# A hybrid encoder layer: the pre-expert weights as 1 MB units in four rotating slots, the first expert gathered transposed, the residual products in the last steps

## The reference, cut to what matters

```
h = rmsnorm(x);  proj = h @ w_in + b_in          # q, k, v, lru-x, lru-gate, merge gates
A = grouped-query attention (8 heads of 64, 2 kv heads, rotary positions)
R = conv4 -> forward and backward gated linear recurrence, summed, times gelu(lru-gate)
x += (sigmoid(gA) * (A @ W_A) + sigmoid(gR) * (R @ W_R)) @ W_out
t = rmsnorm(x);  logits = t @ w_router + b_router
x += sum over the top 4 of 32 experts of gate * (swiglu(t @ w_gu[e] + b_gu[e]) @ w_down[e] + b_down[e])
out = rmsnorm(x)
```

## Time and profile before

| what | value |
|---|---|
| runs | 1136.24, 1137.75, 1137.98 us; median 1137.75 |
| span of the profiled execution, first to last instruction | 1134.2 us |
| around the span (median less span) | 3.55 us |
| TensorE / VectorE / ScalarE busy | 1084.8 / 371.1 / 237.2 us |
| bytes moved by DMA | 439.77 MB, mean 388 GB/s |
| stage before the experts | 0 to 226 us; 32 experts from there on |

### The profile page before, as it was taken

One profiled execution on the slowest core, in us unless ns is written; L12 is line 12 of the kernel. 1 busy time (PEld: TensorE's weight loads), 2 busy tenths in 40 slices (PEclk: granted clock), 3 DMA queues, 4 the chain that ended last, 5 costly groups with the idle time before them and its releaser, 6 DMA issues.

```text
span 1134.2 us, 12887 instructions
## 1 busy us (share of the span) xinstructions
PE 1084.8 (96%) x5407; PEld 503.4 (44%) x5407; DVE 371.1 (33%) x645; ACT 237.2 (21%) x369; POOL 2.6 (0%) x10
## 2 busy tenths in 40 slices
PE   7999999999999999999998989898989899899987
PEld 7999899633333333333333333333333333333332
DVE  6997887522212222122121211111211212121212
ACT  5399961211111111111111110011110101010102
POOL 0000000000000000000000000000000000000000
PEclk9999999899999999999999999999999999999999
DMA  9544277999999999999999999999999999999996
GB/s 353 185 178 149 84 287 300 419 425 399 431 425 428 426 434 432 433 426 435 431 429 436 430 430 436 429 430 436 430 432 433 429 436 430 427 427 429 426 428 247
DMA packets 25637, 439.77 MB, mean 388 GB/s; under 512 B 3425, under 2 KB 4065, under 8 KB 6273
## 3 DMA queue, kind: packets, MB, share of 16 engines
q1 hardware_dynamic: 24976, 438.27, 91.5%
q10 hardware_dynamic: 624, 0.99, 0.2%
HBM read 438.20 MB, written 1.05 MB: 387 GB/s over the span
## 4 chain that ended last, share of the span: by engine, by line
PE 67%; DMA 28%; DVE 2%; SPq 1%; ACT 1%; issue 0%; DVEq 0%
PE ps L1491 26%; DMA slots<-in_w_down_dram 22%; PE ps L1500 13%; PE ps L1172 13%; DMA slots<-in_w_gu_dram 5%; PE ps L1455 5%; PE ps L1436 3%; PE ps L1549 2%; DVE slots_r L725 1%; SPq L403 1%; PE ps L1229 1%; PE ps L1450 1%; PE ps L1414 1%; PE ps L1234 0%; PE ps L1526 0%; PE ps L1274 0%
## 5 line engine op out<-in xcount | busy, mean ns | idle before, releaser
L1500 PE MATMUL ps<-slots,lru 128*64 128x512 f32 x1024 | 239.8, 610 | 17.2 <-DMA slots<-in_w_down_dram 17.2
L1491 PE MATMUL ps<-slots,lru 128*64 128x512 f32 x1024 | 227.7, 594 | 11.7 <-DMA slots<-in_w_gu_dram 11.2
L1491 PE MATMUL ps<-slots,qT 128*64 128x512 f32 x984 | 223.8, 596 | 4.6 <-DMA slots<-in_w_gu_dram 4.6
L1491 PEld LDWEIGHTS ps<-slots,lru 128*64 128x64 f32 x1024 | 74.1, 137 | 160.8 <-issue 139.7
L1491 PEld LDWEIGHTS ps<-slots,qT 128*64 128x64 f32 x984 | 68.9, 137 | 152.2 <-issue 144.8
L1500 PEld LDWEIGHTS ps<-slots,lru 128*64 128x64 f32 x1024 | 68.5, 139 | 142.5 <-issue 123.5
L1100 DVE COPY lru<-ps 128x512 f32<-128x512 f32 x32 | 22.1, 692 | 322.9 <-PE ps L1491 322.9
L1172 PE MATMUL ps<-slots_r 128*128 128x256 f32 (+1 forms) x812 | 107.7, 291 | 0.2 <-DVE slots_r L725 0.2
L1172 PEld LDWEIGHTS ps<-slots_r 128*128 128x128 f32 x812 | 102.2, 191 | 5.4 <-issue 2.5
L653 ACT ACTIVATE lru<-ps 128x512 f32<-128x512 f32 x32 | 19.1, 598 | 395.3 <-PE ps L1491 395.3
L1082 DVE TENSOR_SCALAR lru<-sq,rank_col,small 128x64 f32<-128x64 f32 x64 | 17.2, 312 | 241.8 <-PE ps L1436 241.8
(11 more groups left out here) (200 smaller groups left out, 649.3 us busy)
## 6 DMA issues: line engine op xcount, KB each, us to landing
slots<-in_w_gu_dram SPq DMA_DIRECT2D x40, 4096.0 KB, 29.2
slots<-in_w_gu_dram SPq DMA_DIRECT2D x44, 2048.0 KB, 18.9
slots<-in_w_down_dram SPq DMA_DIRECT2D x20, 4096.0 KB, 28.4
slots<-in_w_down_dram SPq DMA_DIRECT2D x22, 2048.0 KB, 20.8
slots<-in_pre_dram SPq DMA_DIRECT2D x13, 2048.0 KB, 8.2
slots<-in_w_down_dram SPq DMA_DIRECT2D x8, 512.0 KB, 31.0
slots<-in_pre_dram SPq DMA_DIRECT2D x3, 1024.0 KB, 6.9
slots<-in_w_gu_dram SPq DMA_DIRECT2D x3, 1024.0 KB, 17.4
```

The lines of the kernel that those rows point to most:

```text
L1491: ins = nc.tensor.matmul(ps[64 * side:64 * side + 64, 4 + b, :], xgT[i % 2][:, k, :], rows[r][:, o:o + BANK], start=(k == 0), stop=(k == K ...
L1500: ins = nc.tensor.matmul(ps[64 * side:64 * side + 64, bank, :], actT[(i - 1) % 2][:, k, :], w[:, r, side * BANK:(side + 1) * BANK], start= ...
```

## The change

The 15 chunks become 29 units of 1 MB (2048 columns). A unit, its low part in place and its high part lie in one slot together. Units 0 to 5 are in slots 5, 2, 3, 4, 0, 1; from unit 6 on slots 2 to 5 rotate, and slot 6 (`LOWS`) takes units 23 and 28. So slots 0 and 1 are free for the first two expert chunks once q is done, and SyncE issues these behind unit 10. A unit of chunks 1 and 4 to 9 holds all eight row blocks for two groups (256 columns in each, read in runs of 1 KB); of the other chunks, the contiguous first or second half. Each unit has its own split on ScalarE and VectorE, placed anew in their programs. TensorE does all branches before the mix, and ends the mix with the last two blocks instead of the last four.

The first expert's tokens are gathered transposed: x2 is stationary, `sel_next` moves, sixteen products give `xgT` directly in bank 7, which VectorE scales. The copy and the transposes of the first expert go. The four residual products of the router stage and the first step go; the first scatter opens the banks, and the residual is added in two of the last four steps.

```diff
-        PLACE = [2 * (c % PAIRS) for c in range(PRE - 2)] + [LOWS, 4]
+        UNIT = CH // 2
+        UNITS = ([(c, h) for c in range(10) for h in range(1 if c == 3 else 2)]
+                 + [(10, 0), (10, 1), (11, 0), (11, 1), (13, 0), (13, 1), (12, 0), (12, 1), (14, 0), (14, 1)])
+        Q_UNIT, KV_UNIT, BR_UNIT, MIX_UNIT = 4, 6, 19, 25
+        UNIT_SLOT = [5, 2, 3, 4, 0, 1] + [2 + (u + 1) % 4 for u in range(6, 23)] + [LOWS, 2, 3, 4, 5, LOWS]
+        UNIT_FREED = {6: (group_done, 4), 7: (group_done, 4), 8: (group_done, 6), 9: (group_done, 8), 10: (qkv_done, 4),
+                      **{u: (group_done, 2 * u - 12) for u in range(11, 23)},
+                      23: (gate_ps, 32), 24: (branch_ps, 2), 25: (branch_ps, 3), 26: (branch_ps, 4), 27: (branch_ps, 6),
+                      28: (branch_ps, 7)}
+        SLOT_ORDER = [0, 1, 2, 3, 4, 5, LOWS, SLOTS - 1]
+        FREED = {0: (qkv_done, 2), 2: (branch_ps, KD), 3: (mixed_ps, 1), 4: (mixed_ps, 2), 5: (mixed_ps, 3),
+                 LOWS: (mixed_ps, 4)}
-        CAST_V = (5, 9)
+        CAST_V = (9, 10, 17, 18)
...
 SyncE
+            for u in range(4): unit_load(u)
...
+            unit_load(4)
+            unit_load(5)
...
+            for u in range(6, 11): unit_load(u)
+            for k in range(2): expert_load(k)
+            sp.wait_ge(gate_ps, 16)
+            sp.dma_start(ring[LOWS][:, KD * TOK:], w_lru[1]).then_inc(lruw_in, 16)
+            for u in range(11, 22): unit_load(u)
+            sp.wait_ge(rec_ok, 2)
+            sp.wait_ge(pv_ps, NQ // 2)
+            sp.dma_start(late[:, :], expert_src(n, j)).then_inc(extra_full[0], 16)
+            half_load(extra_rows(1, 0), EXTRA[1], 0, extra_full[1])
+            unit_load(22)
+            unit_load(23)
+            half_load(wide[:, 0:2048], 7, 0, slot_full[SLOTS - 1])
+            for u in range(24, 29): unit_load(u)
+            expert_load(2)
+            half_load(wide[:, 2048:], 7, 1, slot_full[SLOTS - 1])
...
 ScalarE
             lru_gates(0, range(4))
             nc.scalar.activation(qk_rstd, qk_rstd, ACT.Sqrt).then_inc(qk_rs, 1)
-            split_high(6)
             for i in range(8, 14):
                 group(i)
                 if i == 9:
                     lru_decay(0, 0)
+                    split_high(11)
                 if i == 11:
                     lru_decay(0, 1)
                     lru_decay(0, 2)
             copy_qk()
             lru_root(0)
+            split_high(12)
             for i in range(14, 16):
                 group(i)
...
-            split_high(7)
+            split_high(13)
             lru_gates(1, [0])
-            split_high(8, [0])
+            split_high(14)
             pair_exps(0)
             lru_gates(1, [1])
             group_pair(16)
-            split_high(8, [1])
+            split_high(15)
             lru_gates(1, [2])
             pair_probs(0)
             pair_exps(1)
             lru_gates(1, [3])
             group_pair(18)
+            split_high(16)
             lru_decay(1, 0)
...
 VectorE
             lru_input(0)
-            split_low(6)
+            split_low(11)
             lru_square(0)
             lru_scaled(0)
+            split_low(12)
             lru_scan(0)
             lru_sum(0)
             pair_max(0)
-            split_low(7)
+            split_low(13)
+            split_low(14)
             pair_norm(0)
             pair_max(1)
-            split_low(8)
+            split_low(15)
             pair_norm(1)
             lru_input(1)
-            split_high(9)
-            split_low(9)
+            split_low(16)
+            split_high(17)
+            split_low(17)
...
             pair_attn(1)
+            split_high(18)
+            split_low(18)
             pair_max(3)
...
-                if g == 1: split_low(12)
-                if g == 3: split_low(13)
-                if g == KD - 1: split_low_by_halves(14)
+                if g != 3:
+                    split_low(22 + g if g < 3 else 21 + g)
...
-            scale_gathered(0, 0)
+            dve.wait_ge(xT_ps, 1)
+            nc.vector.tensor_tensor(xgT[0], ps[:, 7, :].rearrange("p (k n) -> p k n", k=KD),
+                                    g2.unsqueeze(2).to_broadcast([P, KD, CAP]), ALU.mult).then_inc(xg_ok, 1)
...
 TensorE
-            for g in range(4): branches(g)
-            mix(0)
-            for g in range(4, KD): branches(g)
-            for c in range(1, 4): mix(c)
+            for g in range(KD): branches(g)
+            for c in range(ENDS): mix(c)          # ENDS = 6
...
             second_transposes(1)
-            residual_in_bank(0)
             logits(1, range(4))
...
+            def first_gather(t):
+                for k in range(KD):
+                    ins = nc.tensor.matmul(ps[:, 7, k * CAP:(k + 1) * CAP], x2[:, t, k * P:(k + 1) * P], sel_next[:, t, :],
+                                           start=(t == 0 and k == 0), stop=(t == T - 1 and k == KD - 1))
+                return ins
...
-            gather_tile(0)
+            first_gather(0)
             ranks(1)
             pe.wait_ge(sel_ok, T)
-            gather_tile(1).then_inc(xg_ps, 1)
-            residual_in_bank(1)
-            gathered_transposes(0)
+            first_gather(1).then_inc(xT_ps, 1)
...
 step(n, i, first, last, single)
                 if i % 2 == 1:
-                    scatter(1 - i // 2, 2)
-                    scatter(1 - i // 2, 3)
+                    scatter(1 - i // 2, 2, opens)
+                    scatter(1 - i // 2, 3, opens)
+                elif single:
+                    residual_in_bank(i)
+                    residual_in_bank(i + 1)
                 gate_up(n, i, 3, single)
                 if not last:
                     gathered_transposes(n + 1)
-                if first:
-                    residual_in_bank(2)
-                else:
+                if not first:
...
-                if first:
-                    residual_in_bank(3)
-                else:
+                if not first:
```

More of the change, by code:

```diff
@@ L367, in _ @@
             half_load(extra_rows(1, 1), EXTRA[1], 1, extra_full[1])
-            for k in RING_CHUNKS[6:SLOTS]:
+            for k in range(3, SLOTS - 1):
                 expert_load(k)
@@ L513, in _ @@
             act.dma_start(sq[:, 1:, :], squares[:, 1:, :]).then_inc(sq_in, 16)
-            split_high(0)
-            split_high(1)
+            for u in range(4):
+                split_high(u)
             act.wait_ge(lam_e, 1)
@@ L753, in _ @@
             low_part(hT_lo, hT, hT_hi).then_inc(h_lo, 1)
-            split_low(0)
-            split_low(1)
+            for u in range(4):
+                split_low(u)
             dve.wait_ge(lam_e, 2)
@@ L1174, in product, with unit @@
                 return ins
-            def chunk(c, k):
-                return [b.rearrange("p (k n) -> p k n", k=k) for b in (high(c), low(c))]
+            def unit(u, k):
+                return [b.rearrange("p (k n) -> p k n", k=k) for b in (unit_high(u), unit_low(u))]
             def transposes(rows, tp0):
@@ L1202, in first_groups @@
             def first_groups():
-                w = chunk(0, KD)
+                w = [unit(u, 4) for u in range(2)]
                 for q, (a, b, ks) in enumerate(((0, 0, range(4)), (0, 0, range(4, KD)), (0, 1, range(KD)), (1, 0, range(KD)))):
                     if q < 2:
-                        pe.wait_ge(split_hi, q + 1)
+                        pe.wait_ge(*unit_high_ok(q))
                         pe.wait_ge(h_hi, q + 1)
@@ L1239, in _ @@
             for part in range(2):
[L1240 to L1242 removed]
+                pe.wait_ge(*unit_low_ok((Q_UNIT + 1, KV_UNIT)[part]))
+                w = [unit(Q_UNIT, 4), unit(Q_UNIT + 1, 4)] if part == 0 else [unit(KV_UNIT, KD)]
+                per, n_col = (4, QW) if part == 0 else (KD, 2 * KVW)
                 for t in range(T):
@@ L1314, in _ @@
                     values(VALUES_AT.index(i))
-            BLOCKS = CH // P
-            w_br = [chunk(c, BLOCKS) for c in BR_CHUNK]
+            BLOCKS = UNIT // P
+            w_br = [unit(u, BLOCKS) for u in range(BR_UNIT, MIX_UNIT)]
             def branches(g):
                 first = 12 * g
-                for i, c in enumerate(BR_CHUNK[:2]):
-                    if g > 0 and first <= BLOCKS * i < first + 12:
-                        chunk_in(c)
                 if g >= 2:
@@ L1369, in mix_end @@
                     ins.then_inc(mixed_ps, 1)
-            for g in range(4):
+            for g in range(KD):
                 branches(g)
-            mix(0)
-            for g in range(4, KD):
-                branches(g)
-            for c in range(1, 4):
+            for c in range(ENDS):
                 mix(c)
```

275 lines of the change are left out of this document (122 added, 153 removed).

## The result

The changed kernel takes 1149.14 us (median of 4 runs, 1148.02 to 1150.01), the kernel before 1136.99 in the same session: a ratio of 1.0108, 95% interval 1.0093 to 1.0122. That is 12.2 us slower, outside my range. The profiled execution has a span of 1148.1 against 1134.2, so 13.9 us are to be found in the two traces.

The account below looks back on a forecast made before the run. Transfers bound the long run, but TensorE's arrival at the second expert, shifted by d, was taken to set the end. Terms -0.2 + 3.4 + 0.5 - 0.2 - 0.3 - 1.6 = +1.6 gave 1139.4 us, range 1133.5 to 1143.5.

Parts of the forecast that it names:

- start: Opening groups: TensorE's short wait ahead of group 4 goes; -0.2 us, bounds -0.5 and 0.
- splits on the chain, to the third gate block: ScalarE's splits between decays and root delay the scans, so TensorE waits at the second gates; +3.4 us, bounds 0 and 4.5.
- behind that, with the branches: Third probabilities +0.4 us late; in the branches unit 22 holds the third merge about 0.56 us; together +0.5.
- router up to the gather: Router stage: the first residual product goes, where TensorE waited for VectorE anyway; -0.2 us of its 1.7.
- first gather: First gather to first expert matmul: half clock in the first new gather, full in the second; -0.3 us.
- first step: First expert step: two residual products go, so the next expert is released earlier; -1.6 us.
- last steps: Two of the last steps: residual products reappear, covered by waits for transfers; 0 us, up to +1 if uncovered.
- rival D: Slower: new TensorE idle time near 98 to 107 us drops the clock, unit 11 later; +4.1 us, 1141.9, chance 0.21.
- DMA issues: Loads before 200 us: 13 more issues, many in 1 KB runs, cost 0 us but for a late unit 11.
- A: The forecast itself: half clock in the first new gather; +0.5 to +3.5 us, 1138.3 to 1141.3, chance 0.40.
- B: Full clock in the new gather, 2.1 us more gained; -0.5 us, 1137.2, chance 0.17.
- C: Faster: the splits don't reach TensorE, so +3.4 and +0.5 fall away; 1133.3 to 1135.4 us, chance 0.22.

Follow-up runs that it names:

- e1: Changed kernel with SyncE loading units 22 and 23 ahead of the 3 MB of expert weights for late and pbuf; 1150.56 us, ratio 1.0128.
- e3: Changed kernel with the first expert gathered in rows, copied and transposed as before, and two dense products back in the router stage; 1144.08 us, ratio 1.0062.
- e5: Changed kernel with units 22 to 28 loaded ahead of the 4 MB of expert weights for late, pbuf and wide; 1143.05 us, ratio 1.0053.
- e6: Changed kernel with units 11 and 12 loaded ahead of w_lru[1] and the second expert chunk, and both cast on VectorE, not ScalarE; 1139.8 us, ratio 1.0031.
- e8: Kernel before with only the new expert part: transposed first gather, residual products moved to the last steps; weights still in 2 MB chunks; 1136.28 us, ratio 1.0001.
- e7: Changed kernel with the edits of e5, e6 and e3 together; 1134.72 us, ratio 0.9979.
- e12: Changed kernel with only the weight units and their order; router stage, first gather and residual products as in the kernel before; 1147.37 us, ratio 1.0101.
- e4: Changed kernel with eleven more transposes of the identity in TensorE's idle times of the router stage; 1145.05 us, ratio 1.0064.
- e9: Changed kernel with the edits of e5 and e6 together, transposed first gather kept; 1135.61 us, ratio 0.9987.
- e11: e9 with one dense product (x2 with the identity) back ahead of the second logits; 1136.64 us, ratio 0.9992.
- e2: Changed kernel with units 11 and 12 loaded ahead of w_lru[1] and the second expert chunk, and unit 12 cast on VectorE, not ScalarE; 1142.04 us, ratio 1.0048.
- e10: e7 without its two dense products (x2 with the identity) in the router stage; 1136.39 us, ratio 0.9986.

## Why the prediction was wrong

**What held: TensorE's arrival sets the end.** The start of the second expert and the end of each profiled execution:

| kernel | second expert at | end | difference |
|---|---|---|---|
| before | 246.77 | 1134.21 | 887.4 |
| changed | 256.91 | 1148.11 | 891.2 |
| e1 | 260.30 | 1147.79 | 887.5 |
| e3 | 254.68 | 1142.25 | 887.6 |
| e5 | 253.24 | 1140.85 | 887.6 |
| e6 | 250.27 | 1137.90 | 887.6 |
| e8 | 246.58 | 1133.83 | 887.3 |
| e7 | 244.00 | 1132.44 | 888.4 |
| e12 | 256.00 | 1145.43 | 889.4 |

From 246.6 to 260.3 us, 13.7 us of arrival, five of the edits have the end 887.3 to 887.6 behind it, like the kernel before. In e7, the earliest, it is 1 us more, which would fit bytes that begin to count; no run tests it. The changed kernel, e4, e9, e11 and e2 have 889.0 to 891.5, and all five show a half clock in the second expert's first products, as above; it hits work that is already late, behind the point at which I measure. e10 (889.3) and e12 (889.4) show none there; their 2 us stay open (last section).

**Term by term**, in us of d, my forecast and the traces:

| step | forecast | measured |
|---|---|---|
| start | -0.2 | -1.3 |
| splits on the chain, to the third gate block | +3.4 | +6.5 |
| behind that, with the branches | +0.5 | +3.9 |
| mix | 0 | 0 |
| router up to the gather | -0.2 | -0.2 |
| first gather | -0.3 | +0.6 |
| first step | -1.6 | +0.6 |
| last steps | 0 | 0 (e8) |
| sum | +1.6 | +10.1 |

*The splits.* The mechanism was right, the size off, and one part was missing. I took 3.4 and gave 4.5 as the upper bound "if unit 11, queued behind two expert chunks, lands late". It did: ScalarE waited 2.34 us for it, and behind this the whole chain, so that the sum of the scans ended at 100.46 and not near 99. I also counted half of VectorE's move but placed TensorE's wait one block late. Since TensorE came 1.3 us early (it has the lead at the opening gate blocks already; what gave it was not tried apart), the chain took 6.5 us, more than my bound. The bound was under the sum of its parts (3.6 for the scans, and 2.3 for the transfer as it came out). Of the 6.5 the stand itself is 3.77. About 2.6 are the half clock behind it: from the second gate block to the third there are 7.18 us, and 4.60 in the kernel before. The sum had nothing for this.

*The branches.* This is the step that failed. I wrote that the low half of unit 22 holds the third merge "about as long as the old wait there, 0.56 us", with 1.5 as the bound. It held TensorE for 2.95, and the half clock behind this cost 1.55 more. I had seen the 3 MB ahead of it in the queue, and costed the splits but not the transfer: two of those pieces and the unit are 4 MB, some 10 us at 430 GB/s, and the unit, issued at 158.9, landed 9.7 us later, while the units with nothing ahead of them took 5.1 to 6.2. e5 shows it by taking them away; e1 shows that the cost belongs to the queue and not to one unit.

*First gather and first step.* I expected the second gather at full clock and -0.3, "as before the full clock came back at this point". That misread: both gathers of the kernel before take 1.98 us, and where the clock is full the same four records take 1.08 (e7), so it was half for both, and still 0.50 from 222 to 224 us. My own parts for the case, 3.8 + 1.1 + 2.1 + 0.75, also make 7.75 and not 8.15. Both new gathers ran at half and the whole took 9.07, inside my bound of +1.0 for that. What I had not carried on is that the half clock goes on behind the gather: 2.0 us in the first expert's products, which ate the 1.6 that the removed residual products return (1.4 measured: the transposes come 18.47 us behind the first product in the changed kernel and 17.82 before, less 2.01).

*The half clock, over all steps.* About 2.6 us behind the first stand, 1.55 behind the second, 2.0 in the first expert's products and 1.7 in the second's: 7.8 of the 13.9 us. The sum that I forecast by had none of it, and rival D had 1.5. With the late unit 22 this is what made the forecast wrong.

*DMA issues.* They went as forecast. The 78% that I took from the Trainium skill ("DMA: Bandwidth & Descriptors", Bandwidth) is there a share of the peak, of which a 16 MB transfer has 97%. The traces agree that a small transfer is slower for its bytes (1 MB in 5.1 to 6.2 us with nothing ahead of it, the 2 MB chunks of the kernel before in 7.8 to 8.7), and e9's time shows no cost of it.

*The rivals.* D was the right one: a new stand, the half clock, and a late unit. It had a chance of 0.21 and 1141.9 us, one stand and 1.5 us of clock; there were two stands, and the clock fell at four places. The Trainium skill ("TensorE: Matmul & The Clock Gate", "HAM oscillation"), by which I said that D stands and A doesn't, was borne out by these traces: the granted clock fell to 0.5 at each of the two new waits (3.77 and 2.95 us). It doesn't account for e4's profile, in which TensorE stands nowhere in the router stage for more than 0.35 us and the clock falls as before. B, full clock in the gather, is seen in no trace: the first of the two new gathers ran at full clock in e9 (2.18 us), the second never (3.59 us and more). C, splits that don't reach TensorE, is what e6 makes true at the gate blocks, by another order.

*The range.* It went wrong by adding bounds one at a time. Late transfers, longer stands and the half clock behind them hang together here: both stands come, the first of them in part, from loads of the experts put ahead of units that are needed, and they came together.

## What to carry to other kernels

Ask of every transfer that a change lets start earlier what will stand behind it in the queue, and count that queue in bytes; the bytes were not what held the changed kernel, and putting 4 MB of them 37 us later gained 6 us. A split or copy goes where its engine waits anyway (the casts of 1.22 us on the busier VectorE were free, 1.9 us on ScalarE between two links of a chain was not). And behind a wait that a change adds to TensorE, reckon with half clock (each added wait of 1.79 to 6.08 us here had it), and follow it into work that is already late.

## What was not expected of the hardware

Which work in the router stage brings how much half clock isn't settled. By the mean clock from 215 to 245 us, the old gather with dense products had 0.94 in three kernels and 0.89 in the kernel before, every other mix 0.83 or 0.77, with one profile for each, and programs that are the same there differ by up to 0.06. That filling the idle times with small transposes left it at 0.77 was not what I expected.

Executions of one kernel differ, and in two kernels the longest ones have the lowest mean clock: e2's six spans go from 1138.1 (mean clock 0.988) to 1146.3 (0.979), e4's four from 1140.1 (0.985) to 1148.5 (0.981), while e7's eight lie within 1.6. It isn't so everywhere: e12's shortest, 1144.5, has 0.992, but its profiled one is longer by 0.9 at 0.982, and its longest, 1147.6, has 0.988. Two profiles differing by 4 us don't show a change of 4 us; the intervals over several runs do.

Three kernels (the changed one, e4, e12) have a half-clock stretch that begins at 569 to 571 us, and in these the end is 860.8 to 861.2 behind the third expert's start, 2 us more than in the kernel before (858.8), e1, e3, e5 and e6. That is a coincidence in time and no more: e10 and e11 have 860.6 without such a stretch, and no run tested it. The last 2 us of the 13.9 stay open.
